# The output projection one step closer to the scores in an mLSTM stage, and the gate functions moved to a step's first half

## The reference

```python
scores = jnp.einsum('bhcld,bhcsd->bhcls', q, k) * w_intra
num = jnp.einsum('bhcls,bhcsv->bhclv', scores, v) + carry_scale[..., None] * jnp.einsum('bhcld,bhcvd->bhclv', q, c_prev)
den = jnp.sum(scores, axis=-1) + carry_scale * jnp.einsum('bhcld,bhcd->bhcl', q, n_prev)
h = num / jnp.maximum(jnp.abs(den), jnp.exp(-m_t))[..., None]
...
y_ml = jax.nn.sigmoid(ml_o) * _merge_heads(y_ml)
y_ml = _head_rmsnorm(y_ml, ml_norm_w[i], ML_HEADS) * jax.nn.silu(ml_z)
y_sb = _head_rmsnorm(_merge_heads(y_sb), sb_norm_w[i], SB_HEADS) * jax.nn.silu(sb_z)
y = jnp.concatenate([y_sb, y_ml], axis=-1) @ w_out[i]
h = h + _rmsnorm(y, post_norm_w[i])
```

## Time and profile before

| | us |
|---|---|
| median of 3 runs | 1856.84 (1855.57 to 1858.57) |
| profiled execution | 1856.06 |
| its span | 1854.3 |
| TensorE busy | 1775.9 (96%) |
| VectorE busy | 1128.0 (61%) |
| ScalarE busy | 1000.4 (54%) |
| GpSimd busy | 695.9 (38%) |
| mean granted TensorE clock | 0.976 |

### The profile page before, as it was taken

The page is one execution under the profiler, slowest core; times in us unless marked ns, Lnnn a source line. Parts: engine busy times, 40 slices in busy tenths (PEclk is TensorE's granted clock), DMA queues, the critical chain, the costliest instruction groups (busy, mean ns, idle before and its releaser), DMA issues. The chain is left out here.

```text
span 1854.3 us, 28205 instructions
## 1 busy us (share of the span) xinstructions
PE 1775.9 (96%) x8972; PEld 1447.8 (78%) x8972; DVE 1128.0 (61%) x1768; ACT 1000.4 (54%) x2045; POOL 695.9 (38%) x956
## 2 busy tenths in 40 slices
PE   7999999999699999999999999996799999699998
PEld 6888888878378888888788888885688888588887
DVE  5431214554389888878897988785566665433333
ACT  4421213222277787878777778775777775411111
POOL 2100000000146777777767777775243443100000
PEclk9999999999899999999999999997799999899999
DMA  6676765121494637464836485532455553422221
GB/s 192 165 199 194 241 197 162 45 90 46 138 267 141 184 121 235 132 197 131 242 117 186 130 244 177 165 97 85 155 166 180 170 164 125 141 77 77 76 79 43
DMA packets 193381, 277.05 MB, mean 149 GB/s; under 512 B 66716, under 2 KB 128412, under 8 KB 184184
## 3 DMA queue, kind: packets, MB, share of 16 engines
q1 hardware_dynamic: 189592, 259.95, 46.1%
q0 software_dynamic: 3248, 12.62, 1.9%
q10 hardware_dynamic: 432, 3.15, 0.5%
HBM read 187.41 MB, written 88.26 MB: 149 GB/s over the span
## 5 line engine op out<-in xcount | busy, mean ns | idle before, releaser
L948 PE MATMUL b_late<-w_split,spare 128*128 128x512 f32 x1536 | 436.8, 412 | 1.0 <-ACT b_p_out L1030 0.6
L730 POOL TENSOR_TENSOR b_a_lo<-b_aT,b_a_hi 128x512 fp32r<-128x512 f32 (+1 forms) x320 | 367.5, 1149 | 25.6
L1102 DVE TENSOR_TENSOR_SCAN b_buf<-b_y,b_buf 128x511 f32<-128x511 f32 (+2 forms) x320 | 357.8, 1118 | 9.2
L505 PE MATMUL a_po<-uT_hi,w_split 128*128 128x512 f32 x1024 | 318.0, 391 | 2.3 <-DVE w_split L387 2.3
L948 PEld LDWEIGHTS b_late<-w_split,spare 128*128 128x128 f32 x1536 | 265.6, 190 | 43.3 <-issue 1.9
L1112 DVE SCALAR_TENSOR_TENSOR b_buf<-b_buf,b_y 128x512 f32<-128x512 f32 (+2 forms) x320 | 189.2, 591 | 114.4 <-PE b_y L910 112.2
L728 POOL CAST b_a_hi<-b_aT 128x512 fp32r<-128x512 f32 (+1 forms) x320 | 182.4, 570 | 202.3 <-PE b_o L924 155.1
L505 PEld LDWEIGHTS a_po<-uT_hi,w_split 128*128 128x128 f32 x1024 | 192.9, 188 | 46.9 <-DVE w_split L387 2.7
L1016 ACT ACTIVATE b_buf<-b_y 128x512 f32<-128x512 f32 (+2 forms) x320 | 171.4, 536 | 84.6 <-PE b_y L904 82.8
L1007 ACT ACTIVATE b_aT<-b_turned 128x512 f32<-128x512 f32 (+1 forms) x320 | 170.6, 533 | 74.4 <-POOL b_a_lo L730 69.6
L505 PE MATMUL a_po<-uT_lo,w_split 128*128 128x512 f32 x512 | 202.3, 395 | 0.0
(11 more groups left out here) (223 smaller groups left out, 3244.0 us busy)
## 6 DMA issues: line engine op xcount, KB each, us to landing
spare<-u_pair SPq DMA_DIRECT2D x61, 1024.0 KB, 5.4
proj_n<-b_p_out SPq DMA_DIRECT2D x64, 256.0 KB, 5.6
c_gates<-proj_n SPq DMA_DIRECT2D x16, 768.0 KB, 4.5
w_raw<-in_w_in POOLq DMA_DIRECT2D x5, 2048.0 KB, 10.2
x_in<-in_x SPq DMA_DIRECT2D x16, 512.0 KB, 4.0
qk_hi<-stage_hi SPq DMA_DIRECT2D x32, 256.0 KB, 2.5
qk_lo<-stage_lo SPq DMA_DIRECT2D x32, 256.0 KB, 2.9
u_pair<-uT_hi SPq DMA_DIRECT2D x16, 512.0 KB, 3.8
```

Of the source, the lines that this page charges most:

```text
L505: mm = pe.matmul(po[t][:], w[:, k, m * P:(m + 1) * P], u[:, k, t * GROUP:(t + 1) * GROUP], start=(k == 0 and n == 0), stop=(k == KT - 1 an ...
L730: nc.gpsimd.tensor_tensor(lo[:, cols], raw, hi[:, cols].bitcast(F32), ALU.subtract).then_inc(lo_done, 1)
L948: mm = pe.matmul(late[:], u_in[f % US][:, u_part, k, :], w[:, k, :], start=(i == 0), stop=(i == PASSES - 1))
L1102: nc.vector.tensor_tensor_scan(down, y[u % YS][:, 1:keys][:, ::-1], down, b[:, keys - 1:keys], ALU.add, ALU.subtract).then_inc(log_done, 1)
```

## The change

- The lags: `TURN_LAG` goes from 2 to 1, `LAG` (projection and its evacuation) from 3 to 2; a new `POST_LAG` of 3 holds for post norm, residual and store. There are still 19 steps, but TensorE has nothing left in the last.
- TensorE: in step c, `turn(c-1, 0)` stands between the two halves of `project(c-2, 1)`, and `turn(c-1, 1)` behind it, ahead of `combine(c, 1)`. `turn` waits for `sb_y_done` (first half) or `ml_gated` (second half) alone, not both.
- ScalarE: `squash(c)` goes ahead of `evacuate(c-2, 0)` and `weigh(c, 1)`, right behind `square(c-1)`. Both `high` copies stand behind `carry(c, 0)`.
- VectorE: `post` goes from the end of a step to behind the first `weights_times_scores`; both `low` subtractions go behind `numerator(c, 0)`; `norm_heads` is split in two functions that are called in the same place and order.
- GpSimd: `post_norm` ahead of `head_norms`, `add_residual` behind it.
- `c_num` is double, and `numerator` waits for the gating of tile c-2 instead of c-1.
- SyncE: the residual rows `x_in` are loaded by the new `LAG`, the store stands on `POST_LAG`.

The diff, cut:

```diff
-        num = sb("c_num", [P, H, DV + 3])
+        num = [sb(f"c_num{s}", [P, H, DV + 3]) for s in range(2)]
...
-        NORM_LAG, TURN_LAG, LAG = 1, 2, 3
-        FIRST = 2 * LAG
+        NORM_LAG, TURN_LAG, LAG, POST_LAG = 1, 1, 2, 3
+        FIRST = 4
...
             def turn(t, s, half):
-                until(pe, sb_y_done, t + 1)
-                until(pe, ml_gated, t + 1)
+                until(pe, (sb_y_done, ml_gated)[half], t + 1)
...
                 if has(c, 0):
                     score(c, s, 0)
-                if has(c, TURN_LAG):
-                    turn(c - TURN_LAG, st, 0)
                 if has(c, LAG):
                     project(c - LAG, sd, 0)
                 if has(c, 0):
                     score(c, s, 1)
                     combine(c, s, 0)
+                if has(c, LAG):
+                    project(c - LAG, sd, 1, range(KT // 2))
+                if has(c, TURN_LAG):
+                    turn(c - TURN_LAG, st, 0)
+                if has(c, LAG):
+                    project(c - LAG, sd, 1, range(KT // 2, KT))
                 if has(c, TURN_LAG):
                     turn(c - TURN_LAG, st, 1)
-                if has(c, LAG):
-                    project(c - LAG, sd, 1)
                 if has(c, 0):
                     combine(c, s, 1)
...
                 if has(c, 0):
                     weigh(c, 0)
-                if has(c, TURN_LAG):
-                    high(c - TURN_LAG, st, 0)
                 if has(c, NORM_LAG):
                     square(c - NORM_LAG, (s - NORM_LAG) % 2)
+                if has(c, 0):
+                    squash(c, s)
                 if has(c, LAG):
                     evacuate(c - LAG, sd, 0)
                 if has(c, 0):
                     weigh(c, 1)
-                    squash(c, s)
                     carry(c, 0)
+                if has(c, TURN_LAG):
+                    high(c - TURN_LAG, st, 0)
                 if has(c, TURN_LAG):
                     high(c - TURN_LAG, st, 1)
...
             def step(c, s):
+                if has(c, POST_LAG):
+                    post_norm(c - POST_LAG)
                 if has(c, NORM_LAG):
                     head_norms(c - NORM_LAG, (s - NORM_LAG) % 2)
-                if has(c, LAG):
-                    post_norm(c - LAG)
-                    add_residual(c - LAG, (s - LAG) % 2)
+                if has(c, POST_LAG):
+                    add_residual(c - POST_LAG, (s - POST_LAG) % 2)
...
-                until(dve, ml_gated, c)
+                until(dve, ml_gated, c - 1)
...
                 if has(c, 0):
                     weights_times_scores(c, 0)
-                if has(c, TURN_LAG):
-                    low(c - TURN_LAG, st, 0)
+                if has(c, POST_LAG):
+                    post(c - POST_LAG, (s - POST_LAG) % 2)
                 if has(c, NORM_LAG):
                     mean_squares(c - NORM_LAG)
                 if has(c, 0):
                     weights_times_scores(c, 1)
                 if has(c, NORM_LAG):
-                    norm_heads(c - NORM_LAG, (s - NORM_LAG) % 2)
+                    norm_attention(c - NORM_LAG, (s - NORM_LAG) % 2)
+                if has(c, NORM_LAG):
+                    norm_mlstm(c - NORM_LAG, (s - NORM_LAG) % 2)
                 if has(c, 0):
-                    numerator(c, 0)
+                    numerator(c, s, 0)
+                if has(c, TURN_LAG):
+                    low(c - TURN_LAG, st, 0)
                 if has(c, TURN_LAG):
                     low(c - TURN_LAG, st, 1)
                 if has(c, 0):
-                    numerator(c, 1)
+                    numerator(c, s, 1)
                     divide(c, s)
-                if has(c, LAG):
-                    post(c - LAG, (s - LAG) % 2)
```

More of the change, by code:

```diff
@@ L1446, in steps @@
                     step(2 * n + (FIRST + s), s)
-            for c in range(TOK, TOK + LAG):
+            for c in range(TOK, TOK + POST_LAG):
                 step(c, c % 2)
@@ L1486, in step @@
                     sp.dma_start(x_in[sd][:], x[tile(d), :]).then_inc(x_loaded[sd], 16)
-                    if has(c, LAG + 1):
-                        store(d - 1, 1 - sd)
+                if has(c, POST_LAG + 1):
+                    store(c - POST_LAG - 1, s)
                 if isinstance(c, int) and c == TOK + 1:
@@ L1557, in turn, with project @@
                 mm.then_inc(y_turned, 1)
-            def project(d, s, n):
+            def project(d, s, n, ks=range(KT)):
                 until(pe, yT_lo_done, 2 * d + 2)
                 until(pe, out_read, 2 * d - 1 + n)
-                for k in range(KT):
+                for k in ks:
                     for j, (yT, w) in enumerate(((yT_lo, w_hi), (yT_hi, w_lo), (yT_hi, w_hi))):
@@ L1565, in project @@
                                        start=(k == 0 and j == 0), stop=(k == KT - 1 and j == 2))
-                mm.then_inc(out_done, 1)
+                if KT - 1 in ks:
+                    mm.then_inc(out_done, 1)
             def step(c, s):
@@ L1634, in square @@
                 until(act, ml_y_done, b + 1)
-                nc.scalar.activation(squares[:, SB_WIDTH:], num[:, :, 0:ML_DIM], ACT.Square, scale=ML_DIM ** -0.5)\
+                nc.scalar.activation(squares[:, SB_WIDTH:], num[s][:, :, 0:ML_DIM], ACT.Square, scale=ML_DIM ** -0.5)\
                     .then_inc(squares_done, 1)
@@ L1731, in mean_squares, with norm_attention @@
                         .then_inc(ss_done, 1)
-            def norm_heads(b, s):
+            def norm_attention(b, s):
                 until(dve, rstd_done, b + 1)
@@ L1739, in norm_heads, with norm_mlstm @@
                                         ALU.mult).then_inc(scaled_done, 1)
+            def norm_mlstm(b, s):
                 until(dve, silu_done, b + 1)
@@ L1742, in norm_heads @@
                     i = nc.vector.scalar_tensor_tensor(
-                        out=y[s][:, SB_WIDTH + h * ML_DIM:SB_WIDTH + (h + 1) * ML_DIM], in0=num[:, h, 0:ML_DIM],
+                        out=y[s][:, SB_WIDTH + h * ML_DIM:SB_WIDTH + (h + 1) * ML_DIM], in0=num[s][:, h, 0:ML_DIM],
                         scalar=rstd[:, SB_HEADS + h:SB_HEADS + h + 1],
@@ L1747, in norm_heads, with numerator @@
                 i.then_inc(ml_gated, 1)
-            def numerator(c, p):
+            def numerator(c, s, p):
                 u = 2 * c + p
@@ L1752, in numerator @@
                 until(dve, intra_done, u + 1)
-                until(dve, ml_gated, c)
-                nc.vector.tensor_tensor(num[:, 2 * p:2 * p + 2, 0:DV], carried[p][:, :, 0:DV], intra[:, :, 0:DV],
+                until(dve, ml_gated, c - 1)
+                nc.vector.tensor_tensor(num[s][:, 2 * p:2 * p + 2, 0:DV], carried[p][:, :, 0:DV], intra[:, :, 0:DV],
                                         ALU.add).then_inc(num_done, 1)
@@ L1766, in divide @@
                 until(dve, num_done, 2 * c + 2)
-                dens = num[:, :, ML_DIM]
+                dens = num[s][:, :, ML_DIM]
                 nc.vector.scalar_tensor_tensor(out=den[:, 0, :], in0=dens, scalar=-1.0, in1=dens,
@@ L1779, in divide @@
                     i = nc.vector.scalar_tensor_tensor(
-                        out=num[:, h, 0:ML_DIM], in0=num[:, h, 0:ML_DIM], scalar=den[:, 2, h:h + 1],
+                        out=num[s][:, h, 0:ML_DIM], in0=num[s][:, h, 0:ML_DIM], scalar=den[:, 2, h:h + 1],
                         in1=gates[s][:, 2 * GROUP + h * ML_DIM:2 * GROUP + (h + 1) * ML_DIM],
```

## The result

| | before | after |
|---|---|---|
| median | 1856.20 us (4 runs, 1854.86 to 1858.57) | 1902.29 us (4 runs, 1901.31 to 1904.15) |
| profiled execution | 1856.06 us | 1901.31 us |
| span | 1854.3 us | 1899.3 us |
| TensorE busy | 1775.9 us | 1778.5 us |
| mean granted clock | 0.976 | 0.979 |

The account below looks back on a forecast made before the run. TensorE bound the middle at 17.0 us per step; the change would make a 19.5 us cycle of waits. Fourteen of these plus the tail gave +31.8, so 1888; 8 for clock falls made 1896, range 1881 to 1922.

Parts of the forecast that it names:

- The mechanism: Middle steps: early squash on ScalarE delays norm and gate product, so TensorE stands still 2.5 us before each first turning.
- the ring: Closed list of waits from one tile's first turning to the next's, across four engines: 19.5 us against 17.0 of TensorE work.
- Head: First steps: tile 0's division ends at 1305.06, then 9.4 us of waits put turn(0, 0) at 1314.5.
- nine links: Successive work and handovers on TensorE, ScalarE, VectorE and GpSimd between first turnings of successive tiles, together 19.5 us.
- the 2.5: Predicted idle time of TensorE ahead of every turn(c-1, 0), in us.
- link 1: TensorE's four transposes (0.36 us) and twelve matmuls (2.87), so a tile's second turning starts 3.23 us after its first.
- the slack of `low`: First half's low subtraction on VectorE: ready at about 22, under 1 us before TensorE asks at 22.7; no cost expected.
- Tail: Last steps: turn(15, 0) 16.3 us after turn(14, 0), last projection matmul ending at 1620.2.
- The clock: TensorE's clock falls in about two of five steps, each for 1.6 us: 8 us added, forecast 1896; chance 0.60.
- a PEclk under 1.00 in the middle as a sign: Sign expected in the profile after: TensorE's granted clock below full in the middle of the stage.
- The drain of a table load: ScalarE's three table switches: the skill page adds some 1.38 us to each 1.28 us load; rival of 1954, chance 0.01.
- The rival's 58 us: Extra kernel time if each ScalarE table switch also drained, some 4.1 us per step: 1954 in all, chance 0.01.

Follow-up runs that it names:

- two independent cuts of the ring: Changed kernel with squash back behind the second exponentials, 1862.91 us; changed kernel with the norm and gated products ahead of the second weights product, 1866.6 us.
- the first version: Changed kernel with squash behind the second exponentials, residual add on VectorE behind post, mean_squares ahead of both, first high and low ahead of carry and numerator: 1860.84 us.
- the third version: The first version with post and residual add behind the gated products, and tile 15's turning behind tile 14's whole projection: 1854.37 us, ratio 0.9986.
- The two filled kernels: Eight unused matmuls in TensorE's wait before the first turning, added to the residual-first kernel (1890.42 us) and to the changed kernel (1903.58 us).
- the residual-first kernel: Changed kernel with GpSimd's residual add ahead of the head norms instead of behind the gate product: 1902.88 us, ratio 1.0247.
- 3.13 in the second: The first version with step 1's second combine ahead of tile 0's turning, and that step's first high and low behind carry and numerator: 1862.29 us.

## Why the prediction was right, and where its terms were off

The forecast was 1896 and the median 1902.29, inside the range and on the forecast side. The mechanism is confirmed by two independent cuts of the ring. That the number came within 6 us is partly luck: two errors of opposite sign met in it. Step by step:

- **Head.** Forecast: `turn(0, 0)` at 1314.5. Measured: 1314.39. Here, too, two small errors cancel: tile 0's division ended at 1304.26 instead of 1305.06, and the squares of `c_num` began 0.77 us behind it instead of 0.04.
- **Ring.** Its nine links stand in the trace in the order given, and 2.16 to 2.26 us of waiting in most full steps answer to the 2.5. The row of a wait understates what it costs: it is counted from the end of the last matmul (0.40 us long), and without a wait the next one would have begun after 0.23, so 0.17 is to be added. In the first version this explains the 0.4 us per ring above 17.0: waits of 0.19 to 0.27 us, 0.17 on top of each, and 0.05 more from the first to the second turning (3.29 against 3.24 in the third version). But 14 rings took 284.4 us instead of 273 (19.67 the first, then 20.36 on average): +11.4.
- **The mis-sized term** is in link 1, with the four gated products, taken as 2.18 us from before, and the slack of `low`, "under 1 us". They took 4.28, `low` came 0.7 to 0.9 late, and link 1 was 4.2 to 4.35 instead of 3.23. The condition was written in the prediction (the ring would grow by what is missing), but the reason was put at nothing: "The post norm on VectorE and the residual on GpSimd lie in their waits". They do lie in waits of their own engines, but the residual add now follows the gate product on GpSimd directly, beside the products, and lengthens these. The two filled kernels size it at 0.95 us per ring.
- **Tail.** `turn(15, 0)` came 17.2 behind `turn(14, 0)` instead of 16.3, for the same reason, and the end 17.0 behind that instead of 16.4: +1.5.
- **The clock.** Forecast: two falls in five rings, 8 us (its own product, 14 x 0.4 x 1.6, gives 9), and a PEclk under 1.00 in the middle as a sign. In the changed kernel there was no fall in the middle of the stage, and this sign did not come: an error of 8 us that hid two thirds of the other. Without it the sum is 1888 + 11.4 + 1.5 = 1901, the profiled execution's time. In the residual-first kernel, with the same waits, the falls came, 7 in 13 rings at 1.5 us each, where the prediction had priced 1.6. The price was right; the count was a guess, and it failed for this kernel.
- **The drain of a table load.** ScalarE's rows after show 1.28 us per load and the next instruction 0.01 us later, with three loads in the ring, as the earlier trace rows had it. The rival's 58 us did not come.
- **What stays open.** The waits of 2.2 us in the changed kernel and in the residual-first kernel are alike in length, and the same dense projection stands ahead of them. Why the clock fell only in the second was not settled. The kernels differ in the ring's length and in the second wait of 0.9 us that only one has. The length of the wait alone does not decide: ahead of the turning of tile 15, TensorE waited 3.12 us in the first version and 3.13 in the second, and the clock fell to about 0.5 behind the first and stayed at 1.00 behind the second.

## What to carry to other kernels

When a lag between stages is shortened, write down the waits as a closed ring across the engines' in-order lists, with everything that stands ahead of each link on its engine; its sum, not any engine's busy time, is the new step, and here it opened by moving one call out of it. Take a duration from the trace only together with what ran beside it: here an operation moved on GpSimd changed VectorE's durations, and the reverse. If a kernel with expected idle time misses its sum, look at the granted clock in short stretches before you doubt the sum.

## What the hardware showed that was not expected

VectorE and GpSimd hold each other up by what looks like whole instructions. A single gated product takes 0.34 us in the median; the longest is 2.49 us beside the residual add (2.44 us) and 1.36 us where only the gate product (1.30 to 1.34) is beside it. In the other direction GpSimd's 12-column add grew from 0.21 to 1.19 us, and its power from 2.27 to 3.35. The division of the same form into `c_num`, with nothing beside it on GpSimd, takes 1.14 for four. The Trainium skill, "SBUF — State Buffer", section "SBUF: two separate sides", says that a VectorE instruction with two inputs in SBUF and a GpSimd instruction that reads SBUF exclude each other for a whole instruction, and that the later one is blocked. The traces here agree: the longest product is about as long as the GpSimd instruction beside it, and in the first version the 12-column add ends 0.08 us behind `post`.

Eight unused matmuls in a wait of 2.2 us kept the clock at 1.00 and were worth 12.5 us of 1903 in the kernel where it had fallen, and nothing in the kernel where it had not.
